# A gather in two halves ahead of an expert group's products, with another way to rank two experts

## The reference, cut to what matters

```python
x  = x + g1 * (y @ w_out)
h2 = rms(x) * (1 + sc2) + sh2
lg = h2 @ wg + bg                      # 4 groups, the best one is taken
le = h2 @ we + be                      # 32 experts, 8 in each group
top_p, top_i = top_k(softmax(le of the best group), 2)
gate = softmax(lg)[best] * top_p / sum(top_p)
y = sum over the two experts of gate * ((silu(h2 @ w1[e]) * (h2 @ w3[e])) @ w2[e])
out = x + g2 * y
```

## Time and profile before

| | |
|---|---|
| median of three runs | 1605.92 us |
| the profiled execution | 1606.35 us |
| its span, first to last instruction | 1604.5 us |
| TensorE busy, share of the span | 1335.1 us, 83% |
| VectorE busy | 666.7 us, 42% |
| ScalarE busy | 202.5 us, 13% |
| GpSimd busy | 28.7 us, 2% |
| read from memory | 607.13 MB, 380 GB/s over the span |
| mean granted TensorE clock | 0.907 |

### The profile page before, as it was taken

The page is one execution under the profiler, slowest core; times in us unless marked ns, Lnnn a source line. Parts: engine busy times, 40 slices in busy tenths (PEclk is TensorE's granted clock), DMA queues, the critical chain, the costliest instruction groups (busy, mean ns, idle before and its releaser), DMA issues.

```text
span 1604.5 us, 18063 instructions
## 1 busy us (share of the span) xinstructions
PE 1335.1 (83%) x7501; PEld 804.9 (50%) x7501; DVE 666.7 (42%) x852; ACT 202.5 (13%) x502; POOL 28.7 (2%) x32
## 2 busy tenths in 40 slices
PE   6999999999999989989667677678767767767867
PEld 5767888888988858744123123223223213223223
DVE  5768686887676777241121121121122112112212
ACT  3001222221132111211001001001001001001001
POOL 0000000000010000100000000000000000000000
PEclk9999999999999999999788888887788888787879
DMA  9999687856875796999999999999999999999997
GB/s 394 426 425 383 254 328 301 329 220 253 320 307 220 313 374 272 391 405 424 428 428 428 429 428 428 429 428 428 428 429 429 428 428 429 429 428 429 428 429 294
DMA packets 45257, 609.83 MB, mean 380 GB/s; under 512 B 4976, under 2 KB 5504, under 8 KB 6944
## 3 DMA queue, kind: packets, MB, share of 16 engines
q1 hardware_dynamic: 44000, 604.26, 90.1%
q0 software_dynamic: 784, 4.34, 0.7%
q10 hardware_dynamic: 432, 0.65, 0.1%
HBM read 607.13 MB, written 2.10 MB: 380 GB/s over the span
## 4 chain that ended last, share of the span: by engine, by line
DMA 53%; PE 41%; DVE 3%; ACT 1%; issue 1%; SPq 0%; POOL 0%; ACTq 0%; DVEq 0%; POOLq 0%
DMA ring<-in_exp_w 35%; PE W L684 19%; DMA Zpad<-in_exp_w 9%; DMA ring<-in_stream 6%; PE M L1102 5%; PE W L661 3%; DMA tail<-in_exp_w 3%; PE W L985 2%; PE A L1120 2%; PE W L1054 2%; DVE ring L1467 1%; PE W L1067 1%; PE W L638 1%; PE W L1011 1%; PE M L1074 1%
## 5 line engine op out<-in xcount | busy, mean ns | idle before, releaser
L1102 PE MATMUL M<-ring,g1b 128*32 128x512 f32 x1280 | 183.4, 704 | 76.7 <-DMA ring<-in_exp_w 76.5
L1467 DVE CUSTOM_DVE_ANT_0 ring<-ring,tail 128x2048 f32<-128x2048 f32 x96 | 221.3, 2349 | 47.1 <-DMA ring<-in_stream 47.1
L1413 DVE TENSOR_TENSOR consts<-A,tail 32x512 f32<-32x512 f32 x128 | 87.8, 686 | 159.9 <-PE A L1120 156.9
L2011 DVE SCALAR_TENSOR_TENSOR tail<-tail,M 128x128 f32<-128x128 f32 x32 | 9.2, 288 | 299.3 <-ACT tail L1390 299.3
L1102 PEld LDWEIGHTS M<-ring,g1b 128*32 128x32 f32 x1280 | 38.9, 119 | 186.3 <-DMA ring<-in_exp_w 113.5
L684 PE MATMUL W<-ring,buf_x 128*128 128x256 f32 x576 | 128.9, 380 | 0.5 <-DVE ring L1413 0.5
L684 PE MATMUL W<-ring,buf_h 128*128 128x256 f32 x576 | 128.7, 380 | 0.0
L684 PEld LDWEIGHTS W<-ring,buf_x 128*128 128x128 f32 x576 | 108.4, 190 | 16.4 <-DVE ring L1413 0.9
L684 PEld LDWEIGHTS W<-ring,buf_h 128*128 128x128 f32 x576 | 108.6, 190 | 15.4 <-issue 1.1
L1074 PEld LDWEIGHTS M<-consts,tail 128*128 128x128 f32 x512 | 66.6, 203 | 93.2 <-ACT tail L1392 60.3
L1120 PE MATMUL A<-Zpad,tail 128*32 128x512 f32 x512 | 85.1, 795 | 29.3 <-DMA Zpad<-in_exp_w 22.5
(11 more groups left out here) (331 smaller groups left out, 1403.8 us busy)
## 6 DMA issues: line engine op xcount, KB each, us to landing
ring<-in_exp_w SPq DMA_DIRECT2D x96, 2048.0 KB, 36.6
ring<-in_stream SPq DMA_DIRECT2D x86, 2048.0 KB, 13.0
Zpad<-in_exp_w SPq DMA_DIRECT2D x56, 2048.0 KB, 38.0
PPY<-in_exp_w SPq DMA_DIRECT2D x24, 2048.0 KB, 30.6
tail<-in_exp_w SPq DMA_DIRECT2D x16, 2048.0 KB, 45.4
Zpad<-in_early SPq DMA_DIRECT2D x16, 1024.0 KB, 19.5
buf_x<-in_x SPq DMA_DIRECT2D x2, 1024.0 KB, 6.3
buf_h<-in_x POOLq DMA_DIRECT2D x1, 2048.0 KB, 19.7
```

What stands on the lines that cost most here:

```text
L1102: ins = pe.matmul(M[32 * j:32 * j + 32, 512 * w13:512 * w13 + 512], XT[:, kk, 32 * q:32 * q + 32], w[:, 512 * k:512 * k + 512], start=(kk ...
L1413: return dve.tensor_tensor(o, x, y, op)
L1467: ins = dve.tensor_tensor_reduce(w, w, c_rows[:], 1.0, first[:, j:j + 1], ALU.mult, ALU.add, to[:, j:j + 1])
```

## The change

Six edits, in the order of the program:

- The last output block's halves are split by columns: each step of 256 columns needs one half and releases it.
- VectorE makes the diagonals for g2 ahead of the last addition to the residual. SP issues half 9 when the norm's squares and the sums of g2 are done.
- The two best experts come from ranks: for each pair (i, j) of the eight, whether i is above j, or level with it and ahead of it; the sum over i is the rank of j, and a rank under 2 goes into the mask. The two maxima go; the difference of the two logits is taken afterwards.
- The gate weights come behind the first dressing. Where these were waited for, there are new waits: PE's turn of the gates, ScalarE's first tanh of a group, and GpSimd's memsets wait for `g_ready`.
- `gather` and `dress_tokens` take a half (8 of 16 tiles). The first half stands where the whole one stood. The second stands inside the group's first expert.
- The first expert's order is: w1 and w3 with the first half of the rows, second gather, w1 and w3 with the second half, then both sums in turn. The weights' DMAs follow this order.

```diff
             def expert_half(g, j):
                 q, part, hf = j // 6, j % 6 // 2, j % 2
+                if (q, part) in ((0, 0), (0, 1)):
+                    part, hf = hf, part
...
                 elif j == 9:
-                    sp.wait_ge(sem["g2_ready"], 1)
+                    sp.wait_ge(sem["x1_squared"], 5)
+                    sp.wait_ge(sem["g2_summed"], 1)
...
             pool.memset(GT, 0.0).then_inc(sem["gt_ready"], 1)
             pool.wait_ge(sem["gt_ready"], 1)
-            pool.wait_ge(sem["router_done"], 1)
+            pool.wait_ge(sem["g_ready"], 1)
...
                 if n == 3:
-                    w0 = half_arrives()
-                    half[0] += 1
-                    w1 = half_arrives()
-                    half[0] += 1
                     for c in range(2):
+                        w = half_arrives()
                         for kk in range(KT):
-                            w = w0 if kk < 8 else w1
...
+                        half_done(ins)
                         if c == 0:
-                            ins.then_inc(sem["wout_part"], 1)
                             turn_x1(2, range(8, 12))
                             router_wide(1)
-                        else:
-                            ins.then_inc(half_used, 2)
...
-            def gather():
-
-                for b in range(4):
+            def gather(hf):
+
+                for b in range(2 * hf, 2 * hf + 2):
...
             pe.wait_ge(sem["g2_ready"], 1)
-            gather()
-            pe.wait_ge(sem["g_ready"], 1)
+            gather(0)
...
-                            gather()
-                        for w13 in range(2):
-                            for hf in range(2):
-                                if (q, w13) == (0, 0):
...
+                            gather(0)
+                        for i in range(4):
+                            w13, hf = (i % 2, i // 2) if q == 0 else (i // 2, i % 2)
+                            if (q, i) == (0, 2):
+
+                                pe.wait_ge(sem["g2_ready"], 2)
+                                gather(1)
+                            if q == 0 and w13 == 0:
+                                pe.wait_ge(sem["xt_act"], 2 * it + (hf + 1))
+                                pe.wait_ge(sem["xt_dve"], 2 * it + (hf + 1))
+                            w = expert_arrives(pe, it, 6 * q + i)
...
+                            ins.then_inc(half_used, 1)
+                            if i == (3 if q == 0 else 2):
+                                if q == 1:
+                                    pe.wait_ge(sem["gt_ready"], it + 2)
+                                pe.wait_ge(sem["part_copied"], 8 * it + (2 * q + 1))
+                                sum_and_turn(h1T).then_inc(sem["h_turned"], 1)
...
                 ins = act.activation(g2c[32 * m:32 * m + 32, :], W[32 * m:32 * m + 32, 512 * m:512 * m + 512], ACT.Copy)
-            ins.then_inc(sem["g2_ready"], 1)
+                if m % 2 == 1:
+                    ins.then_inc(sem["g2_ready"], 1)
+            def dress_tokens(n, hf):
+
+                act.wait_ge(sem["gathered"], 4 * n + (2 * hf + 1))
+                for k in range(8 * hf, 8 * hf + 4):
...
+            dress_tokens(0, 0)
             act.wait_ge(sem["group_arg"], 1)
...
                     for q in range(4):
-                        act.wait_ge(half_used, PER_GROUP * it + (PE_BASE + 6 * q + 2))
+                        if q == 0:
+                            dress_tokens(it, 1)
+                        act.wait_ge(half_used, PER_GROUP * it + (PE_BASE + 6 * q + (3 if q == 0 else 2)))
                         act.activation(part, M[:, 0:512], ACT.Copy).then_inc(sem["part_copied"], 1)
                         act.wait_ge(sem["h_turned"], 8 * it + (2 * q + 1))
+                        if q == 0:
+                            act.wait_ge(sem["g_ready"], it + 1)
                         act.activation(ee, h1T, ACT.Tanh, scale=0.5).then_inc(sem["e_ready"], 1)
...
+            places = const('iota')[:, 0:EPG]
+            tt_op(ahead, places.unsqueeze(1).to_broadcast([P, EPG, EPG]), places.unsqueeze(2).to_broadcast([P, EPG, EPG]),
+                  ALU.is_lt).then_inc(sem["dve_step"], 1)
...
             residual(3, W[:, 0:512], slice(1536, 1792))
+            dve.wait_ge(sem["ada_half_used"], halves_used(EXPERT_BASE)[1])
+            diagonals(g2_diag, g2_cols).then_inc(sem["diag_ready"], 1)
             item_done(dve, 'wout', 3)
             residual(4, W[:, 512:1024], slice(1792, 2048))
...
-            first_maximum(o1, lev, rt[:, 2:4], EPG)
-            dve.scalar_tensor_tensor(l2, o1, NEG, lev, ALU.mult, ALU.add).then_inc(sem["dve_step"], 1)
-            dve.wait_ge(sem["dve_step"], step_no())
-            first_maximum(o2, l2, rt[:, 4:6], EPG)
+            rank = tie[:, 0:TT * EPG].rearrange("p (a j) -> p a j", a=TT)
+            pairs = [P, TT, EPG, EPG]
+            lev_i, lev_j = lev.unsqueeze(2).to_broadcast(pairs), lev.unsqueeze(3).to_broadcast(pairs)
+            tt_op(level, lev_i, lev_j, ALU.is_equal).then_inc(sem["dve_step"], 1)
+            tt_op(above, lev_i, lev_j, ALU.is_gt)
+            dve.wait_ge(sem["dve_step"], step_no())
+            tt_op(level, level, ahead.unsqueeze(1).to_broadcast(pairs), ALU.mult).then_inc(sem["dve_step"], 1)
+            dve.wait_ge(sem["dve_step"], step_no())
+            tt_op(above, above, level, ALU.add).then_inc(sem["dve_step"], 1)
+            dve.wait_ge(sem["dve_step"], step_no())
+            dve.tensor_reduce(rank, above, AX, ALU.add).then_inc(sem["dve_step"], 1)
+            dve.wait_ge(sem["dve_step"], step_no())
             both = w12.rearrange("p (a j) -> p a j", a=TT)
-            tt_op(both, o1, o2, ALU.add).then_inc(sem["dve_step"], 1)
+            dve.tensor_scalar(both, rank, 2.0, None, ALU.is_lt).then_inc(sem["dve_step"], 1)
...
+            dress_tokens(0, 0)
+
+            dve.wait_ge(sem["group_exp"], 1)
...
+    if arg == 3:
+        return rows_by_partition(w[:, 256 * hf:256 * hf + 256], KT)
```

More of the change, by code:

```diff
@@ L439, in build_program @@
         jdesc = tmp[:, 1760:1792]
+        ahead = tmp[:, 1280:1344].rearrange("p (j i) -> p j i", j=EPG)
+        above, level = (tmp[:, 768 + 128 * i:896 + 128 * i].rearrange("p (a j i) -> p a j i", a=TT, j=EPG) for i in range(2))
         w12 = tmp[:, 1792:1808]
@@ L1091, in _ @@
                             pe.wait_ge(sem["y_added"], 2 * it + 2)
-                            gather()
-                        for w13 in range(2):
-                            for hf in range(2):
-                                if (q, w13) == (0, 0):
[L1096 to L1107, removed]
-                                        pe.wait_ge(sem["gt_ready"], it + 2)
-                                    pe.wait_ge(sem["part_copied"], 8 * it + (2 * q + 1))
-                                    sum_and_turn(h1T).then_inc(sem["h_turned"], 1)
@@ new lines, in _ @@
+                            gather(0)
[8 more added lines that the diff above has]
+                            w = expert_arrives(pe, it, 6 * q + i)
+                            for k in range(8):
+                                kk = 8 * hf + k
+                                j = k % 4
+                                ins = pe.matmul(M[32 * j:32 * j + 32, 512 * w13:512 * w13 + 512],
+                                                XT[:, kk, 32 * q:32 * q + 32], w[:, 512 * k:512 * k + 512],
+                                                start=(kk < 4), stop=(kk >= KT - 4))
+                            ins.then_inc(half_used, 1)
[4 more added lines that the diff above has]
+                                sum_and_turn(h1T).then_inc(sem["h_turned"], 1)
@@ L1396, in _ @@
                         if q == 3:
-                            for b in (0, 2):
-                                act.wait_ge(sem["gathered"], 4 * it + (b + 5))
-                                dress_tokens(b)
+                            dress_tokens(it + 1, 0)
         @block.vector
@@ L1942, in _, with dress_tokens @@
             tt_op(Gm, column(pos3, 0), iob, ALU.is_equal).then_inc(sem["first_ready"], 1)
-            dve.tensor_scalar(pos3[:, :, NE:NE + 4], pos3[:, :, 0:4], -32.0, None, ALU.add)
+            dve.wait_ge(sem["counted"], 1)
+            dve.tensor_reduce(rt[:, 34:35], M[:, 512:512 + NE], AX, ALU.max).then_inc(sem["dve_step"], 1)
+            dve.wait_ge(sem["dve_step"], step_no())
+            dve.tensor_scalar(cnt_i[:], rt[:, 34:35], 31.0, None, ALU.add).then_inc(sem["dve_step"], 1)
+            dve.wait_ge(sem["dve_step"], step_no())
+            dve.tensor_scalar(cnt_i[:], cnt_i[:], 5, None, ALU.logical_shift_right).then_inc(sem["rounds_ready"], 1)
+            def dress_tokens(n, hf):
+                dve.wait_ge(sem["gathered"], 4 * n + (2 * hf + 2))
+                for k in range(8 * hf + 4, 8 * hf + 8):
+                    ins = dve.tensor_scalar(XT[:, k, :], W[:, k * P:k * P + P], gsc[:, KT + k:KT + k + 1],
```

(12 more changed lines are left out.)

52 lines of the change are left out of this document (16 added, 36 removed).

## The result

| | before | after |
|---|---|---|
| median | 1607.03 us, 22 runs (1604.68 to 1611.69) | 1611.11 us, 22 runs (1606.45 to 1615.79) |
| ratio | | 1.0024 [1.0013, 1.0035] |
| the profiled execution, its span | 1606.35, 1604.5 us | 1613.79, 1611.9 us |
| mean granted clock | 0.907 | 0.909 |

The change made the kernel slower by 0.24%, some 4 us. The forecast was 1607.0, no change. It stood on the 1605.92 of three runs, so what it said of the change was 1.0 us; the kernel before came to 1607.03 over 22 runs, and the change measured 4.1 from there.

A forecast was written before the change was run, and what follows sets the result against it. Landing expert weights bound the end, with queue bytes and TensorE's path meeting at h17. 1606.35 + 0.03 (path) + 1.0 (clock) = 1607.4, or 1606.95 from the median; predicted 1607.0, range 1604.2 to 1609.8.

The forecast's parts named there:

- the clock's term: TensorE's clock falls to 1.2 GHz after the sums' stretch ahead of w2: 1.0 us, bounds 0 and 1.6.
- h10: Weight half of 2 MB, used by TensorE in the second expert; forecast issued at 688.6 instead of 694.01.
- everything is as before: From the first w2 product to the use of h10 (scatter, additions, second expert's first four halves), no time changes.
- h17: Weight half that takes h10's place once TensorE has used h10; forecast issued at 728.7, before 728.64.
- The path: TensorE's route to the first product with w2: 702.62 against 702.59 before, +0.03 us.
- c: Start of the last output block's first product, from which times are measured: 642.07 before, 644.38 after.
- stops: Behind each half of the gather, TensorE waits 1.62 us for VectorE's dressing of four tiles.
- The queue: Weight queue's two early dips, 6.0 us together, go and come back as one stall at h17.
- Rival 1: The weight queue keeps what it gains, 6.0 us less: 1600.0; chance 7%.
- Rival 2: TensorE's path is shorter (no clock fall, ranks at their lower end, dressing partly hidden), minus 1.5: 1604.5; chance 15%.
- Rival 3: Second half's dressing waits for GpSimd's memsets, h17 leaves 2.7 us later: 1609.6; chance 8%.
- Rival 4: TensorE's clock falls twice, in the first gather and again at the w2 products: 1609.2; chance 9%.

The follow-up runs named there:

- e1: Changed kernel with another table of places (h17 to place 7, which frees early): 1605.01 us, 0.9979 of before.
- e9: Changed kernel with idle fill products ahead of the second sum and of w2, first expert of a group only: 1609.44 us, 1.0005 of before.
- e10: Changed kernel with idle fill products only behind the halves of the gather: 1608.58 us, 1.0015 of before.
- e5: Changed kernel with idle fill products sized to fit the waits at half gathers, second sum, w2 and scatter: 1607.71 us, 0.9998 of before.
- e11: Kernel before with idle fill products ahead of the second sum, ahead of w2 and in the scatter: 1607.92 us, 1.0000 of before.
- e6: Changed kernel with e5's fill and e1's table of places together: 1602.11 us, 0.9962 of before.
- e12: Changed kernel unaltered, run again beside e9 to e11: 1612.86 us, 1.0025 of before.
- e7: Changed kernel with gather, dressing and first expert's order whole as before, memsets behind the first gather: 1607.91 us, 1.0001 of before.
- e8: e7 with e1's table of places: 1604.78 us, 0.9973 of before.
- e3: Changed kernel with idle fill products at every wait of the first experts, which overran the waits: 1623.5 us, 1.0100 of before.

## Why the prediction was wrong, step by step

**The failed step is the clock's term.** It was priced at 1.0 us with 1.6 as its upper bound. What it left out stands in the sentence that from there to the use of h10 "everything is as before". The profiled execution lost 5.4 on the way to h17: the stretch of the w2 products (706.02 to 712.47) took 6.45 where e1, at full clock, has 3.58, so 2.87; the second sum 0.14 more; the scatter's second step 1.70; the second expert's first w2 half 0.70. The forecast saw the right place (both sums in turn ahead of w2) and allowed one fall of the size that the gather had shown. Two things were missed. The fall was longer: 6.8 us instead of the gather's 3.5. And it wasn't the last: the scatter and the second expert's sums, which before ran at 1.00, fell too. With the sums alone filled they kept their clock, in e9's one profiled execution, and none of its eleven times is a long one. But they don't always depend on the first: in e10's profile the second expert's w2 product fell, and 680 to 720 had no fall.

**The path was right to 0.5 us.** Forecast from c (which was to be 641.71): 86.99 to h17 without the clock's term. Measured without a fall: 87.56 in e5 and e9, and 88.25 - 0.72 = 87.53 in e10. The changed kernel's 92.94 is 87.53 + 5.41. Term by term: start of the gather 39.80 forecast, 39.73 measured; ranks 1.87, 1.82; stops 1.62 each, 1.65 and 1.64; a half of the gather 3.67 (half of the 7.41 in the earlier trace rows is 3.71), 3.84; two products between 3.48, 3.57; from the end of the first expert's products to w2 3.57, 3.66 (e1). The 0.5 is the sum of these small ones.

**The forecast compared against an execution with a fall.** Before's 86.57 holds 1.6 of the gather's fall; e11 without it has 84.95. So at full clock the change makes the path 2.6 longer, not 0.03. The forecast took the lost fall of the gather as a gain that pays for the two stops. That fall did go (1.00 in 680 to 700, before 0.91), but the falls came back elsewhere.

**The queue was right.** The two early dips went but for a rest at 692, the empty stretch moved to ahead of h16 and h17 (of h16 the forecast said nothing), and nothing of the gain was kept. e1 and e6 show that it would be kept with another place for h17, and after h17 no more was lost: from its issue to the end of the span it took 874.6 us, before 875.9.

**The rivals.** Rival 1 was rightly low: it needs the other table. Rival 2 is out, since the path came out longer. Rival 3 is refuted, since the dressing beside the memsets took 1.36. The 1.87 us instruction itself, which now runs ahead of the memsets, took 0.16 (L2012, at 691.75). The Trainium skill's rule ("VectorE: DVE Perf Modes", Why PSUM operands drop a tier, with "SBUF — State Buffer", Who interferes with whom) agrees with this row: by these pages an instruction with its source in PSUM has no mode with both ports, and outside these modes, with one source at most in SBUF, it doesn't contend with GpSimd. They name one more case of contention that the prediction left out, two sources in SBUF beside a GpSimd instruction that reads SBUF; memsets only write. Rival 4, two falls, was the nearest, on the right side and with too low a chance; it put one of them in the gather, where none came.

**The size at the median.** The profiled execution was 7.4 above the one before, the medians 4.1 apart. Eleven of the 22 executions lie at 1612.54 or above (middle one 1613.93), eleven at 1609.67 or below (middle one 1608.62); these differ by 5.3, about the 5.4 of the falls, and the median of 1611.11 lies in the gap between them, so its distance from the forecast depends on how many executions have the falls. That the lower ones are those without the long falls is argued, since no profile of one of them was taken.

**Open.** Why TensorE falls in one execution and not in another of the same kernel, at the same waits. Why executions of the kernel before spread by 7 us although the fill of e11 holds the clock in its sums. Part of the spread lies outside the stretch of the change: c lay between 640.64 and 645.68 in the profiles, and e12's execution, with h17 at nearly the same distance as the result's, needed 2.8 us more from c to its end, with its last w2 product at 2.73 where the result has 1.97. Why e7's median isn't as good as its profile: e8's falls, in the same order, may be the answer, but no slower execution of e7 was profiled. One execution of e8 at 5186.21 us.

## What to carry to other kernels

Before a queue's early stalls are removed, look at the table of places for the next release on the compute path: if that release doesn't come earlier too, the gain is given back there (e1 and e6 kept it by moving one release). When short dependent steps leave TensorE little work on the path, price not one fall of the clock but each such stretch behind it as well, as something that comes in some executions, and compare paths at the same clock, not a path with a fall against one without. Where these waits can't go, idle products sized to fit them hold the clock (e5), but they are worth only what their measured length allows (e3).

## What the runs showed of the hardware

- TensorE fell from 2.4 to 1.2 GHz though its longest idle time there was 0.95 us (ahead of 704.25) and it was busy for 2.5 of the 4 us in 702 to 706; it stayed at 1.2 GHz for 6.8 us, from 706.02 on through products without a gap.
- The falls are not in every execution: e1 and e10, with the same order and the same waits ahead of the second sum and of the w2 product (0.95 and 0.56), ran these at full clock in their profiles; the changed kernel twice did not. e8, with the order of before and waits of 0.72 and 0.56, fell as well.
- A float32 product of 128 rows by 512 columns with full weights takes 0.89 us and leaves two records; one of 256 columns takes 0.46 to 0.49 (2.32 for five in e5 and e11, 1.46 for three in e5).
- A gap of the weight queue has its own cost from issue to flow: with h17 issued at 737.32, the queue moved 8 GB/s in 736 to 738 and 188 in 738 to 740.
